# Zero matmuls in TensorE's first waits, and a new order of the first steps, in a float32 transformer stack on one core

## What is computed

```python
def hybrid_layer(x, ...):
    h = rms_norm(x, pre_g)
    p = split_columns(h @ w_in + b_in)      # w_in: 2048 x about 7000
    ...                                     # four attentions over 256 rows
    return x + rms_norm(mix @ w_out, post_g)
```

## Time and profile before

| | |
|---|---|
| median of 3 runs | 1878.21 us (1876.74, 1878.21, 1882.90) |
| the profiled execution | 1878.3 us, its span 1876.5 us |
| TensorE busy | 1854.4 us, 99% of the span |
| VectorE, ScalarE, GpSimd busy | 1012.6, 858.7, 156.9 us |
| DMA | 338.99 MB, 181 GB/s over the span |

### The profile page before, as it was taken

How to read it: one execution, slowest core, us unless ns; L and a number is a source line. 1 busy time by engine, 2 the same in 40 slices (tenths; PEclk the granted TensorE clock), 3 DMA queues, 4 the chain that set the end, 5 groups by cost and what they waited for, 6 DMA issues and landing times.

```text
span 1876.5 us, 22544 instructions
## 1 busy us (share of the span) xinstructions
PE 1854.4 (99%) x9566; PEld 1588.5 (85%) x9566; DVE 1012.6 (54%) x987; ACT 858.7 (46%) x1066; POOL 156.9 (8%) x168
## 2 busy tenths in 40 slices
PE   8999999999999999999999999999999999999998
PEld 6889988898788998889888888888888888888886
DVE  5545554474753555456475555455455545555544
ACT  6344443464643445346454444454343434435443
POOL 1400011000240001000020000010000101100011
PEclk9999999999999999999999999999999999999999
DMA  8765555455676555446555556554556545456553
GB/s 299 217 194 160 155 186 170 145 183 188 206 213 189 156 158 191 161 128 208 178 186 198 179 179 200 169 181 165 191 168 202 188 158 189 149 165 202 178 181 112
DMA packets 187156, 338.99 MB, mean 181 GB/s; under 512 B 6848, under 2 KB 48688, under 8 KB 186160
## 3 DMA queue, kind: packets, MB, share of 16 engines
q1 hardware_dynamic: 181536, 316.89, 51.8%
q0 software_dynamic: 5232, 20.59, 3.9%
q10 hardware_dynamic: 288, 0.07, 0.0%
HBM read 335.43 MB, written 2.10 MB: 180 GB/s over the span
## 4 chain that ended last, share of the span: by engine, by line
PE 93%; DVE 3%; ACT 2%; DMA 1%; issue 1%; ACTq 0%; DVEq 0%
PE acc L1524 27%; PE acc L1526 27%; PE acc L1525 27%; PE bank L1677 3%; PE bank L1617 1%; DVE w_lo L994 1%; PE bank L1646 1%; PE bank L1666 1%; ACT w_hi L662 1%; PE bank L1885 1%; PE bank L1607 1%; DMA raw<-in_w_in 1%; PE bank L1780 1%; PE acc L1573 0%; PE bank L1635 0%
## 5 line engine op out<-in xcount | busy, mean ns | idle before, releaser
L994 DVE TENSOR_TENSOR w_lo<-raw,w_hi 128x2048 fp32r<-128x2048 f32 (+4 forms) x300 | 660.2, 2203 | 582.2 <-ACT w_hi L662 582.1
L1524 PE MATMUL acc<-w_hi,xt_hi 128*128 128x512 f32 (+4 forms) x2400 | 909.4, 379 | 4.6 <-DVE w_lo L994 4.4
L1526 PE MATMUL acc<-w_hi,xt_lo 128*128 128x512 f32 (+4 forms) x2400 | 902.2, 376 | 0.0
L1525 PE MATMUL acc<-w_lo,xt_hi 128*128 128x512 f32 (+4 forms) x2400 | 901.6, 376 | 0.0
L662 ACT ACTIVATE w_hi<-raw 128x2048 fp32r<-128x2048 f32 (+4 forms) x300 | 542.4, 1810 | 608.5 <-PE acc L1526 590.7
L1524 PEld LDWEIGHTS acc<-w_hi,xt_hi 128*128 128x128 f32 x2400 | 450.9, 188 | 84.0 <-issue 3.7
L1526 PEld LDWEIGHTS acc<-w_hi,xt_lo 128*128 128x128 f32 x2400 | 450.6, 188 | 79.3
L1525 PEld LDWEIGHTS acc<-w_lo,xt_hi 128*128 128x128 f32 x2400 | 451.0, 188 | 77.1 <-issue 0.5
L736 ACT ACTIVATE S<-S,nmax 128x256 f32<-128x256 f32 (+1 forms) x128 | 59.9, 470 | 74.9 <-DVE nmax L1085 49.9
L536 POOL DMA_DIRECT2D bias<-in_b_in x32 | 18.0, 563 | 610.3 <-DVE M L1073 209.9
L723 ACT ACTIVATE PT<-bank 128x512 f32<-128x512 f32 (+2 forms) x76 | 36.3, 554 | 69.6 <-PE bank L1666 52.0
(11 more groups left out here) (287 smaller groups left out, 1266.8 us busy)
## 6 DMA issues: line engine op xcount, KB each, us to landing
raw<-in_w_in SPq DMA_DIRECT2D x76, 1024.0 KB, 5.0
raw<-in_w_in_c SPq DMA_DIRECT2D x64, 1024.0 KB, 5.4
raw<-in_w_in_ab SPq DMA_DIRECT2D x52, 1024.0 KB, 5.1
raw<-in_w_out SPq DMA_DIRECT2D x32, 1024.0 KB, 5.0
raw<-in_w_out_ab SPq DMA_DIRECT2D x16, 1024.0 KB, 5.0
raw<-in_w_out_c SPq DMA_DIRECT2D x16, 1024.0 KB, 5.0
raw<-in_w_in SPq DMA_DIRECT2D x16, 688.0 KB, 4.1
raw<-in_w_in SPq DMA_DIRECT2D x16, 576.0 KB, 3.7
```

What stands on the lines that cost most here:

```text
L994: nc.vector.tensor_tensor(lo[:, :, 0:n], raw[i % RING][:, :, 0:n], hi[:, :, 0:n].bitcast(F32), ALU.subtract).then_inc(lo_done.s, 1)
L1524: nc.tensor.matmul(s, xt_hi[:, kt, rows], hi[:, k, 0:n], start=(q == 0 and k == 0), stop=False)
L1525: nc.tensor.matmul(s, xt_hi[:, kt, rows], lo[:, k, 0:n], start=False, stop=False)
L1526: ins = nc.tensor.matmul(s, xt_lo[:, kt, rows], hi[:, k, 0:n], start=False, stop=(q == NQ - 1 and k == KQ - 1))
```

## The change

A few zeros are written to `tmp` by DVE before its first memsets, with a semaphore of their own. PE multiplies these zeros (128x128 by 128x128, float32, into `bank[3]`, which nothing reads until a later transpose writes it again): nine times before it waits for the identity, three times after `x_cols_t(0)`, and three times after the next set of transposes. `x_cols_t(1)` moves from behind block 0 to ahead of `first_slot`; `x_cols_t(2)` and `x_cols_t(3)` each move one block forward. ACT and DVE split weight piece 0 of chunk 0 ahead of `transposed_half(0, 0)` and no longer behind it. ACT issues the identity's transfer ahead of that of the gains.

```diff
+IDLE = (9, 3, 3)
...
+        zeros_set = signal("zeros_set", 0)
...
+            act.dma_start(cst[:, 0:P], const[:, 0:P]).then_inc(ident_in.s, 16)
             act.dma_start(gT[:, :], gains_t[0]).then_inc(gt_first.s, 16)
-            act.dma_start(cst[:, 0:P], const[:, 0:P]).then_inc(ident_in.s, 16)
             act.wait_ge(ident_in.s, 16)
...
             for i in range(PIECED):
+                if i == 0:
+                    hi_part(i, 0)
                 transposed_half(0, 2 * i)
-                hi_part(i, 0)
+                if i:
+                    hi_part(i, 0)
                 hi_part(i, 1)
...
+            nc.vector.memset(tmp[:, 0:P], 0.0).then_inc(zeros_set.s, 1)
             nc.vector.memset(spare[:, 0:1], 0.0).then_inc(lo_done.s, RING)
...
             for i in range(PIECED):
+                if i == 0:
+                    lo_part(i, 0)
                 transposed_half(0, 2 * i)
-                lo_part(i, 0)
+                if i:
+                    lo_part(i, 0)
                 lo_part(i, 1)
...
                     if k < 2 and q == 0:
-                        x_cols_t(1 + k)
-                    if k == 2 and q == 0:
-                        x_cols_t(3)
+                        x_cols_t(2 + k)
                     if k < 2 and 0 < q < NQ - 1:
                         x_cols_t(2 * q + 2 + k)
...
+            def keep_running(count):
+
+                for _ in range(count):
+                    nc.tensor.matmul(bank[3][:, 0:P], tmp[:, 0:P], tmp[:, 0:P], start=True, stop=True)
+
+            pe.wait_ge(zeros_set.s, 1)
+            keep_running(IDLE[0])
             pe.wait_ge(ident_in.s, 16)
             x_cols_t(0)
+            keep_running(IDLE[1])
+            x_cols_t(1)
+            keep_running(IDLE[2])
             for l in range(DEPTH):
```

## The result

The changed kernel takes 1873.37 us (median of 8 runs, 1871.69 to 1873.99) against 1878.49 us before (8 runs, 1876.74 to 1882.90): the medians are 5.1 us (0.27%) apart, and the ratio taken over all runs is 0.9969, 95% interval 0.9959 to 0.9978. The profiled execution took 1873.99 us with a span of 1872.0 us, 4.5 us under the span of before.

A forecast was written before the change was run, and what follows sets the result against it. TensorE, busy 99% of the span, was taken as the bound. Reaching block 2 at 13.3 instead of 15.83 us gains 2.5 us, so 1878.3 - 2.5 = 1875.8 us; range 1873.4 to 1879.0 us.

The forecast's parts named there:

- slot 1's second chunk: Tightest place after the start, taken by TensorE at 42.51 us before; forecast to come 2.5 us earlier.
- the clock: At the start, TensorE's rise from 1.2 to 2.4 GHz, forecast at 10.85 us, for a gain of 2.5 us.
- w: Time at which TensorE's clock rises to the upper level; forecast 10.85 us, likeliest range 9.5 to 12 us.
- rival (B): Upper clock level before block 0 because the early zeros count: gain 3.6 us, 1874.7 us; chance 16%.
- the prediction's own point: Start of block 2, compared with 15.83 us in the old kernel; forecast near 13.3 us in the new.
- the price of a zero: Zero products before the identity: 0.22 us each at the lower level, nine taking 2.0 us, ending near 3.1 us.
- the bounds: Gain at block 2's start: 1.43 us with the clock rising at 13.05 us, 3.6 us if before real work.
- The identity: Its transfer, issued earlier at 0.81 us, was to land at 4.9 us, putting the first transposes 0.5 us earlier.
- (A): Clock rises as late as before, through a pause at 6.6 us or light zeros: gain 1.4 us; chance 20%.
- (C): Gain lost by slot 1, as a transfer of chunk 4 or 5 doesn't move: no change, 1878.3 us; chance 8%.
- (D): Slower: x_cols_t(1) precedes real work and the second x columns land late; at 10.8 us costs 0.5 us; chance 3%.
- (E): Whole kernel gains more than 0.3%, for which only the spread of runs leaves room; chance 3%.

The follow-up runs named there:

- no_zeros: The changed kernel without any zero products (all three counts 0): 1876.21 us, ratio 0.9984 against the kernel before.
- before_look: The kernel before, unchanged, run again for a second trace: 1877.95 us in one run.
- piece_ident: The kernel before with two edits alone, weight piece 0 split first and the identity transferred first: 1877.08 us, ratio 0.999.
- the kernel of section 6: The changed kernel with zeros (7, 4, 0), x_cols_t(2) and (3) behind blocks 1 and 2, narrow matmuls moved, DVE reordered: 1871.83 us, ratio 0.9968.
- first_zeros: The changed kernel with only the first group of nine zeros (9, 0, 0): 1875.25 us, ratio 0.9983 against the kernel before.
- experiment 2: Here, its run of the kernel before with zeros alone (nine, then three) in the old order: 1875.88 us, ratio 0.9985.
- again: The changed kernel, unaltered, run a second time: 1872.00 us (5 runs), ratio 0.9968 against the kernel before.
- padded: The changed kernel with only the first nine zeros, plus six one-column products ahead of the identity wait: 1872.87 us, ratio 0.9973.

## Why the prediction was wrong

**The reading of the bound held.** TensorE is the bound, and a lead at the start of 3.9 us is still 3.5 us at 580 us. Weight piece 0 landed when forecast, the second part of x at 6.9 us, the third at 9.7 us; block 2's wait of 0.59 us is gone; nothing waits between 20 and 60 us beyond 0.3 us at slot 1's second chunk, the place that the prediction named.

**The step that failed is the clock.** "before, the level rose 3.9 us after unbroken work began; unbroken work now begins at 6.95 us, so w = 10.85 us". In the trace the level was up at 4.47 us. With w ahead of block 0 the sum gives rival (B)'s 3.6 us, and that is what came: at the prediction's own point the chain has block 2 at 12.19 us, 15.83 - 12.19 = 3.6 us. Put otherwise, the sum gave the zeros nothing: its 2.5 us are what the new order brings without them (2.6 us in no_zeros), and the zeros added 1.3 us. Two errors lie under it. The first is the price of a zero: the rows of L1677 count matmuls as the profiler records them, and a float32 product is recorded as two. Nine products so took 3.84 us and not 2.0, filled the whole wait, and left no pause from 3.1 to 5.0 us, which was the reason against (B). The count of zero matmuls after (18 for nine calls) shows it; the earlier trace rows would have shown it before: they have 24 matmuls where the code of L1677 has 12 calls. The second: the 3.9 us were one reading, and counted from unbroken work behind the second x columns. From the start of unbroken work the traces without early zeros have 3.8, 4.8 (before_look), 3.6 (no_zeros) and 5.5 us (piece_ident); with early zeros the level rose 2.9 us (the kernel of section 6) to 5.7 us (first_zeros) after the first of them, 3.3 us in the changed kernel.

The rule cited from the Trainium skill ("TensorE: Matmul & The Clock Gate", Part 1) that the moment differs between runs of one kernel agrees with the traces: the changed kernel's first four transposes took 0.60 us in one and 1.06 us in the other, with the level up from 4.4 and from 6.7 us. What the prediction made of it, a gain anywhere between the bounds, does not hold, since in this order the level is up before block 0 in both and the transfer at 9.7 us hides the rest: block 3 at 13.58 and 13.69 us.

**The identity** landed at 4.15 us, not 4.9, and the first x columns at 4.33 us; the zeros, behind which the transposes start at 4.80 us, hid that.

**What no term held.** 0.95 us come from the load near 580 us, which goes with the length of TensorE's stream. Against that stand 0.2 us lost at slot 1 and 0.2 us in small steps until 580 us. The prediction took the rest of the kernel as unmoved and had every rival end at the start or at slot 1. The last 0.6 us, between 4.5 us of spans and 5.1 us of medians, are the place of two single traces in their bunches: 1878.3 us lies 0.4 us under the mean of the kernel before's middle bunch, 1873.99 us at the top of its own. The second trace agrees: its lead of 6.6 us, less one fall of 1.65 us that before had and it had not, is 5.0 us. The three runs shown of before, 1876.74, 1878.21 and 1882.90, had been read as spread around one value; they were two bunches and a stray. An estimate of the range from the gap between bunches, 1.7 us, would have held the result.

**(A), (C), (D).** (A) is what the old order does with the zeros (experiment 2), behind a pause of 1.9 us (the expectation of first_zeros has 2.5 us, which is the pause of the kernel before, and the fall at 9.7 us, which is 9.45 us). (C) cost 0.2 us here, and 1.1 us in a kernel with a faster start (a lead of 4.92 us at 26 us and 3.80 us at 70 us). The step against it, "each ring issue is released by DVE's split, which moves too", is right of the issue of chunk 4, which moved by 5.1 us, and wrong of its landing, which did not move. (D) stayed out: the second x columns came at 6.9 us, at 7.5 us at the latest seen. With (E)'s 3% the chance for a gain of more than 0.3% was too low for a result that lies at that line (0.27% by the medians, 0.31% by the ratio).

## What to carry to other kernels

Zeros in a wait for first data can lose their worth in the pauses that follow: after a pause of 1.9 us in one order, and after pauses of 0.90 and 0.43 us in one trace of the other, the clock fell again. They should also end when the data comes, since 1 us too many holds up the chain. A faster start is worth only as much as the next transfer leaves: here chunk 4 landed between 25.5 and 27.1 us whatever the start. Before pricing an instruction from a row, hold the row's count against the calls in the code. When a median is split into bunches, look in the trace for the event whose price is their distance: here it was in narrow matmuls 200 us away from the change, and moving eight of them in each hybrid layer took it out.

## What the runs showed of the hardware that was not expected

- One float32 product of 128x128 by 128x128 is two recorded matmuls. Their starts are 0.21 us apart at the lower level and 0.11 us at the upper, so it costs 0.43 and 0.22 us (after, again).
- The granted clock reads 1.00 in the first microseconds although matmuls run at half speed (before, until 13 us); later falls do show, as 0.50.
- The clock fell, by 3.4 us at half speed, while TensorE was busy without a gap: at or just behind 2 us of 15-row products and 0.7 us of 4-column ones, at 8 of 22 places in eleven traces. With full matmuls between the two groups it fell at none of six places in three traces.
- Pauses of 0.2 and 0.94 us ahead of block 0 left the clock up in one trace (first_zeros), and pauses of 0.90 and 0.43 us in another were followed by a fall at 8.3 us (padded). One trace each doesn't tell how often either happens.
- The same 1 MB load took 5.1 to 5.5 or 6.2 to 7.6 us, in an order that follows where the nearest fetch of instructions lies; the length of TensorE's stream long before it moves that place.
